# Splitting each weight unit's high and low parts in two halves, with a semaphore count for each half

## The reference, cut to what matters

```python
def first_block(x, mem, ...):
    x = x + 0.5 * swiglu(rms_norm(x, g1), w_gate, w_up, w_down)        # 1024 -> 2816 -> 1024
    x = x + token_mixing(rms_norm(x, g2), w_in, ..., w_out)            # gated linear attention + convolution
    x = x + memory_cross_attention(rms_norm(x, g3), rms_norm(mem, g4), w_q, w_kv, w_o)   # 256 memory tokens
    x = x + 0.5 * swiglu(rms_norm(x, g5), w_gate, w_up, w_down)
    return rms_norm(x, final_norm)

def second_block(x, meta_tokens, ...):
    h = concatenate([meta, x])
    for i in range(2):
        m = mla_mixer(a, ...) if i == 0 else pool_mixer(a, ...)        # a = rmsnorm(h, ...)
        h = h + rmsnorm(m, ...)
        f = conv_ffn(rmsnorm(h, ...), w_up, conv_w, conv_b, w_down)    # u = h @ w_up, 3 taps over tokens, silu(gate)*val
        h = h + rmsnorm(f, ...)
    return h[:, 16:528]
```

## Time and profile before

| | us |
|---|---|
| median of 3 runs | 2495.24 |
| lowest, highest | 2491.15, 2495.92 |
| the profiled execution | 2494.75 |
| its span, first to last instruction | 2492.9 |
| TensorE busy with matmuls | 2317.0 (93%) |
| VectorE busy | 1167.5 (47%) |
| GpSimd busy | 893.1 (36%) |
| ScalarE busy | 874.9 (35%) |

### The profile page before, as it was taken

The page is one execution under the profiler, slowest core; times in us unless marked ns, Lnnn a source line. Parts: engine busy times, 40 slices in busy tenths (PEclk is TensorE's granted clock), DMA queues, the critical chain, the costliest instruction groups (busy, mean ns, idle before and its releaser), DMA issues.

```text
span 2492.9 us, 35005 instructions
## 1 busy us (share of the span) xinstructions
PE 2317.0 (93%) x14099; PEld 2026.6 (81%) x14099; DVE 1167.5 (47%) x1584; ACT 874.9 (35%) x1302; POOL 893.1 (36%) x404
## 2 busy tenths in 40 slices
PE   8999999998979999999978999799999848999998
PEld 6888887777766678888777888799999837999998
DVE  4323245365523442232456554662635576626355
ACT  4222234314423242222354443442423335323233
POOL 2444444321352234444431112234343332343432
PEclk9999999989999999999989999899999968999999
DMA  5333323321332123333311012132323201323231
GB/s 147 93 93 97 97 80 92 84 60 47 88 121 65 53 83 94 97 96 93 92 44 31 23 35 60 47 89 85 93 85 90 72 17 51 91 87 93 85 87 66
DMA packets 355681, 193.57 MB, mean 78 GB/s; under 512 B 7357, under 2 KB 350034, under 8 KB 355554
## 3 DMA queue, kind: packets, MB, share of 16 engines
q1 hardware_dynamic: 355026, 190.61, 26.3%
q10 hardware_dynamic: 528, 1.19, 0.1%
HBM read 189.67 MB, written 2.10 MB: 77 GB/s over the span
## 4 chain that ended last, share of the span: by engine, by line
PE 66%; DVE 19%; ACT 8%; issue 4%; POOL 1%; DVEq 1%; DMA 0%; ACTq 0%; SPq 0%; POOLq 0%
PE PS L528 17%; PE PS L530 17%; PE PS L532 17%; DVE u_conv L892 4%; DVE g_conv L892 2%; ACT w_hi L481 2%; PE PS L550 2%; PE PS L1950 2%; POOL w_lo L471 1%; PE PS L1968 1%; DVE u_conv L895 1%; ACT u_conv L845 1%; DVE hid L903 1%; ACT g_conv L833 1%; ACT h_hi L848 1%
## 5 line engine op out<-in xcount | busy, mean ns | idle before, releaser
L471 POOL TENSOR_TENSOR w_lo<-raw,w_hi 128x1024 fp32r<-128x1024 f32 (+3 forms) x389 | 871.4, 2243 | 1548.8 <-ACT w_hi L481 1548.8
L528 PE MATMUL PS<-XHI,w_hi 128*128 128x512 f32 (+2 forms) x2632 | 741.4, 332 | 44.3 <-DVE XLO L628 37.7
L530 PE MATMUL PS<-XLO,w_hi 128*128 128x512 f32 (+2 forms) x2632 | 730.5, 328 | 0.0
L481 ACT ACTIVATE w_hi<-raw 128x1024 fp32r<-128x1024 f32 (+3 forms) x389 | 379.5, 981 | 1000.1 <-PE PS L532 928.0
L532 PE MATMUL PS<-XHI,w_lo 128*128 128x512 f32 (+2 forms) x2632 | 728.2, 327 | 0.0
L528 PEld LDWEIGHTS PS<-XHI,w_hi 128*128 128x128 f32 x2632 | 445.8, 190 | 104.3 <-issue 48.6
L530 PEld LDWEIGHTS PS<-XLO,w_hi 128*128 128x128 f32 x2632 | 443.6, 189 | 45.8 <-issue 2.6
L532 PEld LDWEIGHTS PS<-XHI,w_lo 128*128 128x128 f32 x2632 | 444.5, 190 | 43.3
L528 PE MATMUL PS<-h_hi,w_hi 128*128 128x512 f32 (+2 forms) x1056 | 283.6, 323 | 12.0 <-DVE h_lo L905 8.5
L530 PE MATMUL PS<-h_lo,w_hi 128*128 128x512 f32 (+2 forms) x1056 | 281.6, 321 | 0.0
L532 PE MATMUL PS<-h_hi,w_lo 128*128 128x512 f32 (+2 forms) x1056 | 281.5, 321 | 0.0
(11 more groups left out here) (294 smaller groups left out, 2370.7 us busy)
## 6 DMA issues: line engine op xcount, KB each, us to landing
raw<-in_ffn_w_up SPq DMA_DIRECT2D x132, 512.0 KB, 3.8
raw<-in_ffn_w_down SPq DMA_DIRECT2D x64, 512.0 KB, 3.9
raw<-in_ffn_w_gate SPq DMA_DIRECT2D x44, 512.0 KB, 3.8
raw<-in_w_in SPq DMA_DIRECT2D x25, 512.0 KB, 3.8
raw<-in_ffn_w_down SPq DMA_DIRECT2D x32, 384.0 KB, 3.4
raw<-in_xattn_w_kv SPq DMA_DIRECT2D x16, 512.0 KB, 3.9
raw<-in_w_out SPq DMA_DIRECT2D x8, 512.0 KB, 3.7
raw<-in_xattn_w_q SPq DMA_DIRECT2D x8, 512.0 KB, 3.8
```

What stands on the lines that cost most here:

```text
L471: ins = nc.gpsimd.tensor_tensor(d, r, h.bitcast(F32), ALU.subtract)
L481: ins = nc.scalar.activation(d, r, ACT.Copy)
L528: nc.tensor.matmul(ps, wh, ahi(k)[:, c:c + w], start=(k == 0), stop=False)
L530: nc.tensor.matmul(ps, wh, alo(k)[:, c:c + w], start=False, stop=False)
```

## The change

For units without a form the slice of a unit is now two slices, the first and the second half of its columns (k = 0 to 3 and 4 to 7, or the two contraction tiles of a value unit). ScalarE copies a half and signals, then the other half and signals; GpSimd waits for a half, subtracts it and signals, then the same for the other. `hi_done` and `lo_done` now rise by two per unit; units with a form are handled as before and signal 2 at once. TensorE waits for the count of the first half ahead of a unit and for that of the second ahead of its tile k = kt/2. SyncE waits for both halves, as before. Three places wait on whole units still: the mixer's output units (line 1175 before), the latent attention's jobs (1934) and the pooling's units (2230).

```diff
--- before.py
+++ after.py
@@ -426,7 +426,8 @@
                      w_hi[:, s, c].rearrange("p (g m) -> p g m", m=NOPE)) for t, c in enumerate(cut)]
         if u.form is None:
             w = u.kt * u.cols
-            return [(dst[:, s, 0:w], raw[:, r, 0:w], w_hi[:, s, 0:w])]
+            cut = (slice(0, w // 2), slice(w // 2, w))
+            return [(dst[:, s, c], raw[:, r, c], w_hi[:, s, c]) for c in cut]
         g = u.kt * u.cols // P
         d = dst[:, s, 0:g * P].rearrange("p (g m) -> p g m", m=P)
         h = w_hi[:, s, 0:g * P].rearrange("p (g m) -> p g m", m=P)
@@ -439,10 +440,14 @@
 
         return n + add if isinstance(it, int) and it == 0 else 4 * it + (n + add)
 
+    def halves(n, it, add, half):
+
+        return 2 * (n + add) + half if isinstance(it, int) and it == 0 else 8 * it + (2 * (n + add) + half)
+
 
     def sp_unit(sp, n, it, u):
         if n >= RAW or not (isinstance(it, int) and it == 0):
-            sp.wait_ge(lo_done, later(n, it, 1 - RAW))
+            sp.wait_ge(lo_done, halves(n, it, 1 - RAW, 0))
         sp.dma_start(raw_view(n, u), u.src(it)).then_inc(raw_loaded[n % RAW], 16)
 
     def walk(eng, step):
@@ -465,11 +470,15 @@
 
 
     def pool_unit(pool, n, it, u):
-        pool.wait_ge(hi_done, later(n, it, 1))
         pieces = hi_lo_pieces(n, u, w_lo)
         for i, (d, r, h) in enumerate(pieces):
+            if u.form is None or i == 0:
+                pool.wait_ge(hi_done, halves(n, it, 0, i + 1 if u.form is None else 2))
             ins = nc.gpsimd.tensor_tensor(d, r, h.bitcast(F32), ALU.subtract)
-        ins.then_inc(lo_done, 1)
+            if u.form is None:
+                ins.then_inc(lo_done, 1)
+        if u.form is not None:
+            ins.then_inc(lo_done, 2)
 
 
     def act_hi(act, n, it, u):
@@ -479,7 +488,10 @@
             act.wait_ge(unit_summed, later(n, it, 1 - SPLIT))
         for d, r, _ in hi_lo_pieces(n, u, w_hi):
             ins = nc.scalar.activation(d, r, ACT.Copy)
-        ins.then_inc(hi_done, 1)
+            if u.form is None:
+                ins.then_inc(hi_done, 1)
+        if u.form is not None:
+            ins.then_inc(hi_done, 2)
 
     hi_next = [0]
 
@@ -517,9 +529,13 @@
         if wait:
             if n >= 4 or not (isinstance(it, int) and it == 0):
                 pe.wait_ge(unit_read, later(n, it, -3))
-            pe.wait_ge(lo_done, later(n, it, 1))
         s = n % SPLIT
+        there = 0
         for k in ks or range(u.kt):
+            need = 1 if k < u.kt // 2 else 2
+            if need > there:
+                pe.wait_ge(lo_done, halves(n, it, 0, need))
+                there = need
             if ready:
                 ready(k)
             c0 = k * u.cols + cols0
@@ -1074,9 +1090,9 @@
         dve_mix.wait(pe, ("min", 3))
         for i in range(4):
             m = n + 5 + i
-            pe.wait_ge(lo_done, m + 1)
             s = m % SPLIT
             for kk in range(2):
+                pe.wait_ge(lo_done, 2 * m + kk + 1)
                 k = 2 * i + kk
                 wh, wl = w_hi[:, s, kk * 512:(kk + 1) * 512], w_lo[:, s, kk * 512:(kk + 1) * 512]
                 for t in range(4):
@@ -1172,7 +1188,7 @@
 
         u = FLAT[n]
         pe.wait_ge(unit_read, n - 3)
-        pe.wait_ge(lo_done, n + 1)
+        pe.wait_ge(lo_done, 2 * (n + 1))
         s = n % SPLIT
         for at, k in enumerate(MIXO_ORDER):
             ready(at)
@@ -1931,7 +1947,7 @@
         if before >= 0:
             job_wait(pe, JOBS[before], n, job_read, unit_read)
         m = n + job.unit
-        pe.wait_ge(lo_done, m + 1)
+        pe.wait_ge(lo_done, 2 * (m + 1))
         s, bank = m % SPLIT, job_bank(job)
         if job.kind == "v":
             for i, j in enumerate(job.at[1]):
@@ -2227,7 +2243,7 @@
         for k in range(KD):
             pe_square(pe, S_POOL, SUMS, 2, k)
         for g in range(4):
-            pe.wait_ge(lo_done, n + g + 1)
+            pe.wait_ge(lo_done, 2 * (n + g + 1))
             s = (n + g) % SPLIT
             for k in range(2):
                 pe.wait_ge(x_lo, KD * D_POOL + 2 * g + k + 1)
```

## The result

| | before | with the change |
|---|---|---|
| median of the runs, us | 2493.19 (2489.36 to 2495.92, 4 runs) | 2460.49 (2459.45 to 2468.25, 4 runs) |
| ratio to before | | 0.9872, 95% interval 0.9858 to 0.9886 |
| profiled execution, us | 2494.75 | 2468.25 |

The first experiment repeats the kernel and its profile shows one of the usual ones (2458.44), so both are read here.

A forecast was written before the change was run, and what follows sets the result against it. TensorE, busy 2317.0 of 2492.9 us, bounds the kernel; gain only where it stands for a weight unit. 5.1 + 2.0 + 2.0 + 9.1 + 4.8 + 2.0 - 1.0 = 24.0, thus 2471 us, range 2463 to 2488.

The forecast's parts named there:

- the sum of 24: All seven terms of the prediction added, gains less costs: 24.0 us off the whole kernel.
- part 6: Start of down parts: the tap that a subtraction blocks ends earlier, 0.2 to 0.5 each, together 2.0 us.
- Part 1: Cross attention, keys and values: the low part 1.55 us earlier removes all the excess of late units, 5.1 us.
- Part 2: Cross attention, VectorE: each of two `XLO` waits for a half only, about 1.8 for 2.8 us; 2.0 together.
- Part 3: Mixer, unit 75: first half ready at 443.8 where the whole subtraction ended at 445.76; gain 2.0 us.
- Parts 4 and 6: Convolution feed-forwards and fourth units lose all their excess, 9.1 us; starts of down parts get a shorter blocked tap, 2.0.
- Part 5: Ends of phases: the last `acc` ends 1.5 us earlier at four ends, 0.4 at one of them; 4.8 us.
- Part 7: Costs: 0.10 us for each added copy ahead of something critical on ScalarE, ten places, -1.0 us.
- VectorE does get between the halves: Rival denied this: GpSimd goes straight on, only the earlier signal counts, 15.2 us, 2480; chance 0.22.
- no wait appeared in mid-unit: Rivals: TensorE stops in mid-unit, gain given back, 2490 to 2495, 0.11; mid-unit waits break its flow, at worst 2538, 0.06.
- the change does what it says: Rival denied this: a remaining wait on whole units sits where the gain is, 2480 or above; chance 0.03.
- a satisfied wait costs nothing: TensorE's 354 added waits: nothing taken for them, since weight loads at unit starts follow by 0.23 us as elsewhere.

The follow-up runs named there:

- The first experiment: The changed kernel once more, unaltered: 2459.42 us (2458.42 to 2467.49, 4 runs), ratio 0.9872.
- the satisfied wait: Kernel before, with a second wait for the same, already reached count on TensorE in mid-unit, about 300 in all: 2494.89 us, ratio 1.0003.
- the 14 matmuls: Kernel before, with 14 small matmuls, result unread, in TensorE's stand ahead of each norm sum at the four last phases' ends: 2493.76 us, ratio 0.9996.
- the change with only the mixer filled: Full change plus 16 matmuls of 512 columns, result unread, where TensorE stands in the mixer before unit 89: 2459.23 us (2451.86 to 2462.77, 6 runs).
- the kernel before with all stands filled: Kernel before (whole units) plus unread matmuls in TensorE's stands in the mixer and at five phase starts: 2482.79 us, ratio 0.9958.
- Filled stands: Full change plus unread matmuls in TensorE's stands in the mixer and at five phase starts: 2453.19 us (2450.86 to 2458.72), ratio 0.9839.

## Why the prediction was right or wrong

Direction and mechanism were right, the size was not: the sum of 24 missed 9. Two steps failed: **the sum had no term for TensorE's clock**, which carries 6 to 7 of the 9, and **part 6 was too small**, by 3 us at two places. The first is seen when executions of the same mean granted clock are set against each other (the 84 executions of the kernel before that were timed beside the experiments, and the eight of the change; means in us, number of executions in brackets):

| granted clock of the execution | before | with the change | difference |
|---|---|---|---|
| 0.968 | 2494.1 (32) | 2467.9 (2) | 26.2 |
| 0.971 | 2487.0 (4) | 2459.6 (6) | 27.4 |

At equal clock the change gains 26 to 27 us, near the 24 of the sum. The other 6 to 7 of the 33 are that six of eight executions have 0.971 with the change, and only eight of 84 have that or more before. The profiled executions say the same: by the trace's clock intervals, matmuls ran at 1.2 GHz for 88 us before, 89 in the change and 68 in the repeat; the distances are 26.5 and 36.3, and 20 us less at half clock are worth up to 10. Why the change's executions mostly have the higher clock isn't shown. By its parts, against the repeat, which holds that clock:

- **Part 1, keys and values**, 5.1: measured 5.3. Units 107 to 115 each start 0.9 to 1.1 earlier against the last, and stand for nothing; value units start 5.60 apart where the earlier trace rows had 6.74. Right, and three entries of that row show why: +0.1 without halves there, +0.6 with halves and one signal, -2.2 where TensorE waits for the whole.
- **Part 2, the `XLO`**, 2.0: measured 0.9 to 1.3. In the change three `XLO` alternate with halves of GpSimd:

```profile
685.46 9.33 DVE L644 SCALAR_TENSOR_TENSOR XLO<-X,cols,XHI 128x512 fp32r<-128x512 f32 x8
...
689.61 6.31 POOL L477 TENSOR_TENSOR w_lo<-raw,w_hi 128x512 fp32r<-128x512 f32 x4 [3.04 <-ACT w_hi L490]
```

  The two engines block each other half by half (four halves take 6.31 where 4 x 1.28 are 5.1), and unit 106's copy comes early enough to join. That the blocked `XLO` becomes shorter was right; that there would be as few of them was not.
- **Part 3, unit 75**, 2.0: measured 2.4 at the unit itself, with unit 76 3.1. Here the one profile of before misleads: the kernels with the satisfied wait and with the 14 matmuls, which leave unit 75 alone, have 1.0 less in this row as well. Set against those, the change gives 2.1 in this row and 3.4 over 70 to 78.
- **Parts 4 and 6, convolutions, fourth units and down parts**, 9.1 + 2.0: measured 7.1 + 7.6 + three fourth units of 0.36, 0.36 and 0.47, 15.9. The term that failed here is part 6. I counted the tap of `u` alone. The chain before a down part is longer: VectorE's tap of the gate, its read of `u`, ScalarE's first tap behind a copy, VectorE's tap of `u`. At the second down part, before and with the change:

```profile
1827.15 1.50 DVE L892 SCALAR_TENSOR_TENSOR g_conv<-g_buf,cols,g_conv 128x528 f32<-128x528 f32 x1 [1.01 <-ACT g_conv L833]
...
1829.48 0.70 DVE L887 TENSOR_TENSOR u_buf<-PS,rn 128x528 f32<-128x528 f32 x1
...
1831.10 0.82 ACT L845 ACTIVATE u_conv<-u_buf,cols 128x528 f32<-128x528 f32 x1
...
1832.06 2.16 DVE L892 SCALAR_TENSOR_TENSOR u_conv<-u_buf,cols,u_conv 128x528 f32<-128x528 f32 x1 [1.88 <-ACT u_conv L845]
```

```profile
1810.72 1.34 DVE L908 SCALAR_TENSOR_TENSOR g_conv<-g_buf,cols,g_conv 128x528 f32<-128x528 f32 x1 [1.01 <-ACT g_conv L849]
...
1813.67 0.71 DVE L903 TENSOR_TENSOR u_buf<-PS,rn 128x528 f32<-128x528 f32 x1 [0.70 <-PE PS L548]
...
1814.79 0.82 ACT L861 ACTIVATE u_conv<-u_buf,cols 128x528 f32<-128x528 f32 x1
...
1815.75 1.80 DVE L908 SCALAR_TENSOR_TENSOR u_conv<-u_buf,cols,u_conv 128x528 f32<-128x528 f32 x1 [1.37 <-ACT u_conv L861]
```

  Before, the read of `u` starts 1.30 us behind TensorE's first matmul of unit 267 (1828.18) with no idle ahead of it, since VectorE was late; with the change it starts 0.20 behind (1813.47) and waits for TensorE. `h_lo` ends 9.35 behind that matmul before, and 7.39 now. Of these 1.96 the earlier read is 1.10, ScalarE's tap, which the copy ahead of it delays less, 0.51, and the two taps of `u` on VectorE, 0.35. The forecast's 0.3 is this last one, and it was right; the 1.6 ahead of it were missing. The step to unit 268 is 1.88 us shorter, that to 340 1.84, where 0.3 each was forecast, 3.1 of the 4.8 by which these parts are short; 289 and 361, 0.97 each, were forecast so. The rest is spread over other units.

  A subtraction in halves isn't enough for this. VectorE is busy 98 us less for the same 1584 instructions, but so it is with one signal for a unit, where the step to unit 268 is only 0.39 shorter: there the read of `u` starts 1.11 behind TensorE (1832.23 against 1831.12), 0.19 earlier than before and not 1.10. With GpSimd starting at the first half and TensorE waiting for both the step is 1.89 shorter. So it is GpSimd's earlier start with the halves that brings the chain forward; by which of the instructions before unit 267 isn't singled out. The Trainium skill (GPSIMD Engine Reference, 1. Specifications) says that the two engines share their interfaces to SBUF and contend where VectorE's instruction has two inputs there; the rows agree (the read of the gate out of PSUM at 1809.01 takes 0.70 beside halves that start at 1808.83, the tap with two inputs in SBUF 1.80 to 2.16 beside a subtraction and 0.77 without one).
- **Part 5, ends of phases**, 4.8: measured 2.44 (unit 201) and 3.0 (227 and 228). `acc` fell from 2.41 to 0.82 us as forecast (1.5). The missing clock term shows here in one place: the norm sum takes 1.10 us and not 2.04 with a shorter stand ahead of it, 0.94 more at the end of the second feed-forward. The experiment with 14 small matmuls, with VectorE's chain as before, shows that what TensorE does in that stand sets it.
- **The clock elsewhere.** Rows 70 to 73 and 117 to 126 of the table give 1.5 and 4.3 us in the repeat, 5.8 in all, and the forecast had nothing there. In the stretch from 790 to 830 us the granted clock is 0.87 before, 0.96 in the profiled execution of the change and 1.00 in its repeat. This isn't the halves by themselves: the change with only the mixer filled has 0.87 there again and 0.1 in the row 117 to 126, and the kernel before with all stands filled gains 4.2 in it. And the kernel with the satisfied wait starts unit 72 1.5 us earlier as well, and loses 1.3 of it at unit 73.
- **Part 7, costs**, 1.0: measured 0.6 at unit 89. Another 0.7 was lost from 202 to 228, but the kernel before with 14 small matmuls loses 0.8 there too (units 208 and 209), so this isn't shown to be a cost of the halves. The two copies take 1.13 to 1.15 us, by 0.08 more than the one of 1.056, not by 0.19: where the page of the Trainium skill quoted in the prediction gives an estimate of 1.9 us for the term, the trace stays with the row.

In sum for the repeat: 5.3 + 1.3 + 3.1 + 15.9 + 5.4 - 1.3 = 29.7, with 5.8 of clock and 0.8 in the rest 36.3, the distance of the two profiled executions (2494.75 less 2458.44). The range ended at 32 since its best case added a larger part 6 and half a microsecond for part 3, and took no clock and no spread of the executions.

Of the rivals: VectorE does get between the halves (`acc`), no wait appeared in mid-unit, and the change does what it says. That a satisfied wait costs nothing, which the sum took from the unit starts, is shown.

## What to carry to other kernels

Cutting a producer's instruction in two pays where its consumer misses by less than the half and can be signalled by halves: cut with one signal, the same instructions gave nothing (0.9999). Where a second engine is blocked by it, follow that engine's whole chain to the next stand, not the one blocked instruction next to it. Put a term for TensorE's clock into every sum that shortens a stand, but count only the time at 1.2 GHz in which TensorE works: 39 of the 44 us that fillings took away had cost nothing. Where executions of one kernel differ in granted clock, compare executions of equal clock, and profiled ones stretch by stretch, before a cause is named.

## What was not expected of the hardware

- Two matmuls of 512 columns in f32 took 2.04 us behind a stand of 4.26 us and 1.10 behind one of 2.76.
- The same program lost or kept 5 us in one stretch of the mixer; the granted clock there was 0.66 and 1.00 over 20 us.
- The kernel before takes 2494.1 us at a mean granted clock of 0.968 and 2487.0 at 0.971.
- Some 300 satisfied waits between matmuls cost nothing that 12 runs show (ratio 1.0003, 0.9993 to 1.0013).
- Filled stands made 138 us at 1.2 GHz 93, and 39 of the 44 us lay where TensorE stood anyway; the kernel with them has the lowest median here, 2453.19 us against 2459.42 of the repeat, with ranges that touch.
